# Hybrid decoder step in float32: the end of each layer's expert stage rearranged

## The reference, cut to what matters

```python
for i in range(2):
    h = h + mixer(rmsnorm(h))                  # layer 0: convolution, layer 1: latent attention
    h = h + hier_moe(rmsnorm(h))               # 32 experts of width 256, two per token
    h = h + (p[i] @ ple_w_in[i]) * sigmoid(rmsnorm(h, ple_g[i]) @ ple_w_gate[i])
return rmsnorm(h, norm_final), ...
```

## Time and profile before

| | |
|---|---|
| median of 3 runs | 794.77 us (792.7 to 796.37) |
| span of the profiled execution, first to last instruction | 790.0 us |
| TensorE busy | 93% of the span |
| VectorE busy | 43% |
| ScalarE busy | 26% |
| mean granted TensorE clock | 0.981 |
| end of the experts, layer 0 and layer 1 | about 342 us and 740 us |

### The profile page before, as it was taken

One profiled execution on the slowest core, in us unless ns is written; L12 is line 12 of the kernel. 1 busy time (PEld: TensorE's weight loads), 2 busy tenths in 40 slices (PEclk: granted clock), 3 DMA queues, 4 the chain that ended last, 5 costly groups with the idle time before them and its releaser, 6 DMA issues.

```text
span 790.0 us, 16349 instructions
## 1 busy us (share of the span) xinstructions
PE 731.0 (93%) x6292; PEld 523.9 (66%) x6292; DVE 341.6 (43%) x1014; ACT 204.8 (26%) x499; POOL 55.0 (7%) x99
## 2 busy tenths in 40 slices
PE   9999999999999679899999999999999997688994
PEld 7886677666676446658876567777766665365583
DVE  2688624433333113235456865253333332233355
ACT  2200323421112101132235653145222121111232
POOL 2401000000000000000052630000000000000000
PEclk9999999999999989999999999999999998999997
DMA  8972995999999999999268775999999999999801
GB/s 331 395 243 72 311 426 207 390 424 420 426 428 426 423 431 424 414 421 402 111 214 288 249 226 203 427 428 376 393 423 428 425 429 423 427 430 413 344 1 55
DMA packets 48769, 271.18 MB, mean 343 GB/s; under 512 B 6817, under 2 KB 17265, under 8 KB 28465
## 3 DMA queue, kind: packets, MB, share of 16 engines
q1 hardware_dynamic: 41520, 258.50, 80.6%
q10 hardware_dynamic: 4272, 6.88, 2.6%
q0 software_dynamic: 2896, 4.72, 1.9%
HBM read 262.71 MB, written 3.88 MB: 337 GB/s over the span
## 4 chain that ended last, share of the span: by engine, by line
PE 47%; DMA 21%; DVE 4%; SPq 4%; issue 3%; ACT 2%; POOL 0%; POOLq 0%; ACTq 0%; DVEq 0%
PE bank L652 13%; DMA ring<-in_moe_w_gate_up 11%; PE bank L816 11%; DMA arena<-in_moe_w_gate_up 6%; PE bank L772 6%; PE bank L845 4%; DMA arena<-in_moe_w_down 4%; PE bank L859 3%; SPq L2337 2%; SPq L2341 2%; PE bank L789 1%; PE bank L1153 1%; PE bank L586 1%; PE bank L988 1%; PE bank L870 1%
## 5 line engine op out<-in xcount | busy, mean ns | idle before, releaser
L816 PE MATMUL bank<-ring,arena 128*32 128x256 f32 x1344 | 109.2, 399 | 16.9 <-DMA ring<-in_moe_w_gate_up 13.8
L652 PE MATMUL bank<-arena,ring 128*128 128x264 f32 (+1 forms) x440 | 102.4, 388 | 0.3 <-DVE arena L1690 0.3
L652 PE MATMUL bank<-xn_sq,ring 128*128 128x264 f32 x448 | 100.9, 386 | 0.0
L816 PEld LDWEIGHTS bank<-ring,arena 128*32 128x32 f32 x1344 | 58.5, 115 | 56.5 <-issue 33.2
L1537 DVE TENSOR_TENSOR arena<-arena,bank 128x128 f32<-128x128 f32 x34 | 9.8, 288 | 197.6 <-ACT arena L1995 197.6
L652 PEld LDWEIGHTS bank<-xn_sq,ring 128*128 128x128 f32 x448 | 85.0, 190 | 15.3 <-issue 0.9
L652 PEld LDWEIGHTS bank<-arena,ring 128*128 128x128 f32 x440 | 82.8, 190 | 17.2 <-issue 3.0
L772 PEld LDWEIGHTS bank<-arena 128*128 128x128 f32 x768 | 87.9, 192 | 8.3 <-issue 8.3
L772 PE MATMUL bank<-arena 128*128 128x128 f32 (+1 forms) x768 | 91.2, 277 | 0.0
L1555 DVE TENSOR_TENSOR hT<-hT,bank 128x264 f32<-128x264 f32 x144 | 61.6, 429 | 20.6 <-PE bank L870 11.8
L859 PE MATMUL bank<-arena 128*128 128x264 f32 x256 | 63.6, 393 | 3.0 <-issue 3.0
(11 more groups left out here) (293 smaller groups left out, 888.9 us busy)
## 6 DMA issues: line engine op xcount, KB each, us to landing
ring<-in_moe_w_gate_up SPq DMA_DIRECT2D x32, 2048.0 KB, 18.7
ring<-in_stream SPq DMA_DIRECT2D x34, 1024.0 KB, 13.8
arena<-in_moe_w_gate_up SPq DMA_DIRECT2D x14, 2048.0 KB, 24.3
ring<-in_moe_w_down SPq DMA_DIRECT2D x26, 1024.0 KB, 21.3
arena<-in_moe_w_down SPq DMA_DIRECT2D x26, 1024.0 KB, 22.1
xn_sq<-in_moe_w_gate_up SPq DMA_DIRECT2D x12, 2048.0 KB, 20.9
ring<-in_moe_w_gate_up SPq DMA_DIRECT2D x12, 1024.0 KB, 22.8
shelf<-in_moe_w_down SPq DMA_DIRECT2D x8, 1024.0 KB, 22.1
```

Of the source, the lines that this page charges most:

```text
L652: t = mm(ps[:, 0:cols], lhs(k), rhs(k), start=(k == 0), stop=(k == n - 1))
L816: t = mm(bank[2 + r][p0:p0 + U, 0:F].rearrange("p (c f) -> p c f", c=2), x, w[i][:, :, k * F + c * P:k * F + (c + 1) * P], start=(k == 0), ...
```

## The change

On TensorE the five products ahead of the branch go. The last pair's two halves are copied by two engines: ScalarE makes the first, VectorE the second, ahead of its branch. The scaling of `xnT` moves from VectorE to ScalarE, which now makes eight scalings as the additions come and all eight squares behind them. In `embed` the sums of the squares no longer stand inside chunk 0 but in one piece (`sum_parts`) behind chunk 1, and the all-ones product goes from ahead of chunk 2 to ahead of chunk 3. Both layers are changed alike.

```diff
@@ -930,7 +930,6 @@
                 turn_hid(NPR - 1)
                 combine(NGR - 2, (KD - 1,))
                 down(NPR - 1)
-                fill_in(bank[3], 5)
 
                 pe.wait_ge(s_perm, l + 1)
                 with pe.If(pe.value_load(mostI[0:1, 0:1], min_val=0, max_val=NSLOTS) > 0):
@@ -980,23 +979,27 @@
             def embed(l, norm):
 
                 key = "n2" if l == 0 else "n5"
-                sums = open_bank(pe, (key, "parts"))
                 first = open_bank(pe, ("pg", l, 0))
                 landed(pe, G_PG[l])
                 for i, k in enumerate(LASTK):
                     pe.wait_ge(s_xn, KD * norm + i + 1)
                     t = mm(first[:, 0:T], slot(G_PG[l]).rearrange("p (k f) -> p k f", k=KD)[:, k, 0:P], xnT[:, k, :],
                            start=(i == 0), stop=(i == KD - 1))
-                    if i == KD - 1:
-                        t.then_inc(is_full(("pg", l, 0)), 1)
-                    if i % 4 == 3:
-                        for r in range(4):
-                            pe.wait_ge(s_sq, SQ[key] + i - 2 + r)
-                            t = mm(sums[32 * r:32 * r + 32, 0:T], ones[:, 0:32], sq[:, LASTK[i - 3 + r], :],
-                                   start=(i == 3), stop=(i == KD - 1))
-                t.then_inc(is_full((key, "parts")), 1)
+                t.then_inc(is_full(("pg", l, 0)), 1)
+
+                def sum_parts():
+
+                    sums = open_bank(pe, (key, "parts"))
+                    for i, k in enumerate(LASTK):
+                        pe.wait_ge(s_sq, SQ[key] + i + 1)
+                        t = mm(sums[32 * (i % 4):32 * (i % 4) + 32, 0:T], ones[:, 0:32], sq[:, k, :], start=(i < 4),
+                               stop=(i >= 4))
+                    t.then_inc(is_full((key, "parts")), 1)
+
                 for m in range(1, KD):
                     if m == 2:
+                        sum_parts()
+                    if m == 3:
                         freed(pe, (key, "parts"))
                         chunk(key, 1, lambda k: ones, lambda k: rstd[:])
                     g = G_PG[l] + m // 2
@@ -1579,16 +1582,15 @@
                 hidden(NPR - 1)
                 for k in (KD - 2, KD - 1):
                     add(NGR - 2, k)
+                q = NPR - 1
+                dve.wait_ge(s_dn, pb + NPR)
+                v.tensor_copy(O[64:P, q // 2 % 2, 512:D], bank[4 + q % 2][64:P, :]).then_inc(s_out, 1)
 
                 with dve.If(dve.value_load(mostI[0:1, 0:1], min_val=0, max_val=NSLOTS) > 0):
                     general(l)
 
-                for i in range(KD + 1):
-                    if i < KD:
-                        add(NGR - 1, i)
-                    if i:
-                        dve.wait_ge(s_add, KD * (gb + NGR - 1) + i)
-                        gained("ple_g", KD * l, LASTK[i - 1])
+                for i in range(KD):
+                    add(NGR - 1, i)
 
             def general(l):
 
@@ -2007,7 +2009,7 @@
                     act.wait_ge(s_dn, pb + q + 1)
                     if j >= 2:
                         act.wait_ge(s_cb, KD * (gb + j - 1))
-                    for h in range(2):
+                    for h in range(1 if q == NPR - 1 else 2):
                         p0 = 64 * h if q == NPR - 1 else 64 * r
                         s.copy(O[p0:p0 + 64, j % 2, 512 * h:512 * (h + 1)], bank[4 + r][64 * h:64 * h + 64, :])\
                          .then_inc(s_out, 1)
@@ -2070,6 +2072,8 @@
 
                 for i, k in enumerate(LASTK):
                     act.wait_ge(s_add, KD * (gb + NGR - 1) + i + 1)
+                    s.mul(xnT[:, k, :], hT[:, k, :], vcol("ple_g", KD * l + k)).then_inc(s_xn, 1)
+                for k in LASTK:
                     s.activation(sq[:, k, :], hT[:, k, :], ACT.Square).then_inc(s_sq, 1)
                 key = "n2" if l == 0 else "n5"
                 ps = arrive(act, (key, "parts"))
```

## The result

The changed kernel takes 802.04 us (median of 15 runs, 797.72 to 807.97), the kernel before 798.37 us in the runs made beside it (median of 15, 792.7 to 801.55). The ratio is 1.0074 with a 95% interval of 1.0048 to 1.0099: slower by 0.7%, on the side that the prediction held likeliest. On 798.37 us, 799.6 is only 0.15% more, and the absolute time is low by 2.4 us. The mechanism that was to decide came true; the terms for the clock and for the branch did not, and that the ratio agrees so well is in part luck. (The recorded ratios are not quotients of the medians: 802.04/798.37 is 1.0046.)

What follows compares the result with a forecast made beforehand. VectorE, not TensorE, was taken to set the embedding's end. Moved sums, less interruptions, shorter combine and branch, gave +2.84 us in layer 0 and, after slack, +1.99 in layer 1: 794.77 + 4.83 = 799.6 us, range 794.5 to 803.0.

Steps and rivals of the forecast that it cites:

- One more chunk of products lies ahead of it: Moved sums: the all-ones product waits for one more chunk, 3.59 us, less an estimated 0.15 for two interruptions gone.
- C: The start of the last combine at a layer's end, 743.38 in layer 1 before; forecast 0.1 us sooner.
- rival 1: Ahead of the last combine: the branch only drained TensorE's queue, so C comes 2.2 us earlier; 795.4 us; chance 0.18.
- C - down: Time from the start of the last down product's second half to C; forecast to change by -0.1 us.
- one packet of the instruction queue goes out 0.6 us after TensorE's branch begins: Branch ahead of the last combine: TensorE starts again 2.5 us after the packet, read as a 3.1 us wait for code.
- rival 2: Gap left by the unused products: TensorE's clock falls, 2.5 us a layer; 804.6, or 802.1 if in one; chance 0.15.
- 2.8 lies between, nearer the first: TensorE's 2.8 us gap lies between 2.16 us (64 matmuls took 3.66) and 4.24 us (clock 0.50, they took 6.17).
- the first gate product 2.9 after the combine's start: Sign behind the last combine: gate products at C + 2.86 instead of C + 3.39, 0.5 us earlier.
- The 2.5 us of the earlier trace: Extra time of 64 matmuls at half clock behind a 4.24 us gap: 6.17 us against 3.66.
- the whole +2.84: Layer 0: VectorE's later embedding start reaches the next stage in full, +2.84 us, as its product waited for VectorE.
- V8: VectorE's eighth step (L1680) of the embedding; forecast +2.84 us in layer 0, +1.99 in layer 1 after 0.85 slack.
- without idle: Layer 0 embedding: VectorE goes from its start at 361.01 to its eighth L1680 at 380.45 without idle.

Runs made afterwards that it cites:

- Experiment 2: The kernel before with only the part sums moved behind chunk 1 and the all-ones product ahead of chunk 3: 803.76 us, ratio 1.0058.
- experiment 1: The changed kernel with the all-ones product right behind the part sums, ahead of chunk 2 instead of chunk 3: 797.17 us, ratio 0.9998.
- experiment 9: The changed kernel with TensorE's branch two groups earlier and nothing else: 796.89 us, ratio 1.0017 to the kernel before.
- experiment 4: The changed kernel with 2 and 4 unused products in TensorE's gap in the next stage's first chunk behind layer 0: 804.03 us, ratio 1.0087.
- Experiment 5: The changed kernel with TensorE's part of the overflow body cut to its last wait: 796.13 us, ratio 0.9991 to the kernel before.
- experiment 7: The kernel before with TensorE's branch two groups earlier, without the unused products, copies by two engines: 790.15 us, ratio 0.9927.
- experiment 8: The changed kernel with the all-ones product right behind the part sums and TensorE's branch two groups earlier: 790.58 us, ratio 0.9919.
- experiment 10: The kernel before with TensorE's branch two groups earlier, without the unused products, both copies by ScalarE: 791.75 us, ratio 0.9958.
- experiment 3: The changed kernel with the five unused products back ahead of the branch: 802.41 us, ratio 1.0045 to the kernel before.
- experiment 6: The kernel before without its five unused products, all else as before: 799.94 us, ratio 1.0044.

## Where the prediction held, and which of its steps failed

**What held.** "One more chunk of products lies ahead of it" decided. The all-ones product comes 3.22 us later behind the gate products (11.79 - 8.57), where 3.59 - 0.15 = 3.44 was forecast, and VectorE keeps its 3.22 us behind it. Experiment 2 has a loss of the same size with this part alone, in experiment 1 one line takes the loss away, and experiment 9 has it with the branch out of play. That C is not 2.2 us sooner without the unused products, so that rival 1 is out, held as well (C - down -0.28 and +0.07, forecast -0.1), but in this execution only: in experiments 1 and 4, also without the products, C came those 2.2 us sooner in three layers, because the branch was short. Experiment 5 shows that the length of the body and not the queue's drain makes the wait. Additions 0.40 us apart (3.22/8, forecast 0.34), eight scalings in 3.50 us (each lasts 0.50 as forecast, but they overlap and follow each other at 0.44), copies in parallel, an all-ones product 12.0 after the gate products (11.8): the steps around it stand. VectorE's start moved by 3.31 us against the down product in layer 0 and by 3.55 in layer 1, its eighth step by 3.09 and 2.71: layer 1 absorbed 3.55 - 2.71 = 0.84, where 0.85 was forecast.

**The step that failed: the branch as a constant.** I took 3.03 and 3.17 us, two values of one execution, for what a branch over this body costs, and "one packet of the instruction queue goes out 0.6 us after TensorE's branch begins" for a sequence of cause and effect. In the other profiles the same branch took 0.42 to 5.59 us. In all 22 branches over a long body that the profiles hold, the end lies 2.4 to 2.8 us after the last packet of that queue (q8), but over this body the packet left from 2.3 us before the branch started to 3.1 us after. So what the unused products hide differs from run to run. Most of the spread goes with it: with the short body or the early branch the standard deviation of the runs is 1.1 to 2.3 us (experiments 5 and 7 to 10), with the long branch at its old place 2.3 to 4.4 (after 3.3, experiments 1 to 4 and 6). A base of three runs under such a spread was 3.6 us off, and the absolute forecast with it. The Trainium skill, "Runtime: NRT & Kernel Launch", section "Instruction fetch mechanics", has a taken branch outside the fetched pages stall for a fetch. Experiments 5 (0.2 us over a few instructions, no packet near it) and 7 (6.2 us over the larger body, 2.5 us of it behind a packet) agree. It doesn't tell the 0.42 from the 5.59 over one body.

**The second step that failed: the clock, which the sum had at nothing.** "TensorE's clock falls in the gap" stood as rival 2, with a chance of 0.15 and 2.5 us a layer. It did fall in both layers, behind 2.77 and 3.07 us of idle time, so the judgement "2.8 lies between, nearer the first" was wrong, and with it the sign "the first gate product 2.9 after the combine's start" (3.73 and 3.65). In this execution it cost 0.8 us a layer and not 2.5, because it was full again after some 3.4 us: where -0.5 was forecast from the combine, +0.34 and +0.26 was measured. The 2.5 us of the earlier trace rows were the price of 64 matmuls that kept TensorE busy for 6.17 us at the half clock. That the price stayed at 0.8 was the luck of the draw: where the clock fell in the other executions, VectorE's start came later against C by 1.4 us (experiment 3, layer 0), 2.0 (experiment 1, layer 1), 2.9 (experiment 10, layer 0) and 2.9 and 3.25 (experiment 6), with the half clock lasting some 3.4, 6.8 and 10 us; so rival 2's price was of the right order. A third fall, ahead of the next stage, had no term in the sum and no rival: VectorE's late start leaves TensorE idle for 1.28 and 2.07 us with one product between, and that costs 1.68 us. The prediction let "the whole +2.84" arrive in the next stage and asked nothing about TensorE's wait there. The unused products had a second worth, to hold the clock over a wait of some 3 us (experiment 3), for which the prediction gave them no credit.

**The sum.** Forecast: +2.84 in layer 0 and +1.99 in layer 1, 4.83 in all. Measured in the profiled execution: 3.09 + 1.68 + 2.71 = 7.48; 2.65 more. In layer 0 the combine gave 0.84 less than forecast (the clock), the moved sums cost 0.19 less, C came 0.18 sooner, and 0.22 was taken up by V8 (its third step took 3.84 us instead of 4.07: VectorE waits there for a square by ScalarE, which issues three DMAs first, a wait that the prediction's "without idle" passed over): +0.25. In layer 1 it is +0.76 - 0.22 + 0.17 + 0.01 = +0.72. The third fall of the clock adds 1.68. By the medians it is 802.04 - 798.37 = 3.7 us, by the ratio of 1.0074 some 5.9. So the pair of profiles shows a larger loss than the runs do, and the ratio came out near the forecast although terms of 1.68 and twice 0.8 us were missing. A part of this can be told. In every profiled execution whose own time is known, time less span is 1.6 us; by that (an estimate) the profiled execution of the kernel before took 791.7 us, 6.7 below its median of 15, while that of the changed kernel lies 0.9 below its own. Longer branches with the clock falling behind them can make the kernel before that much slower: from the down product to VectorE's start it is 19.3 us in its profile and 24.85 in experiment 6's layer 0. Which of them its median execution had, no profile shows. The cleanest pair, experiments 7 and 9, has the branch out of play: 5.9 us by the trace and 6.7 by the medians, where these terms were forecast at 5.03.

**What stays open.** What decides when the packet of code leaves. Whether unused products make it leave sooner. Why 1.29 us of idle time once cost the clock and once did not. Also open are the 2.0 us of span that lie where nothing was changed.

## What to carry to other kernels

Before products are moved, ask which engine sets the end of the stretch, and what its start waits for: here one chunk of TensorE's work ahead of a sum cost 3.2 us a layer, and every operation that was made cheaper meanwhile gave nothing measurable. A long branch body on the engine that sets the end is a wait of unknown length; put the branch ahead of a wait that is there anyway (0.4% here, 0.7% with the second copier) or keep the body short. Count with such a wait also the clock of the work behind it: here up to 3.25 us more. And read a cost that stands once or twice in a trace as a draw: compare a second execution, or the spread of the runs, before it becomes a term of a sum.

## What the runs showed of the hardware that was not expected

- A branch over the overflow body took 0.42 to 5.59 us, one over a few 0.21 to 0.24, one over the larger body of the early branch 5.84 to 6.38. But for the few-instruction ones, the end lay 2.4 to 2.8 us after a packet of the instruction queue.
- The half clock came behind gaps of 2.60, 2.77, 3.07, 4.62 and 5.74 us, behind 1.28 and 2.07 us with little between, and once behind 1.29. In the changed kernel's first two gaps the clock was still full for nearly the whole gap and half behind it. The half clock lasted some 3.4 us in the changed kernel, 6.8 in experiments 1 and 10 and 10 us in both layers of experiment 6, and cost 0.8 to 3.25 us up to VectorE's start. "TensorE: Matmul & The Clock Gate", Part 1, of the Trainium skill says that the phase of the clock gate is not tied to the kernel and that its effect varies from run to run; experiment 10's two layers agree.
- A copy of 64x512 from one PSUM bank takes 0.58 us on ScalarE and 0.69 on VectorE, also when both read the same bank at once (ScalarE its first 64 partitions, VectorE the other 64).
